# Prompt attention in a hybrid decoder layer: mask added inside VectorE's maximum, exponentials taken in place, copies and exponentials in turn on ScalarE

## The reference, cut to what matters

```python
s_own = jnp.einsum('tcgd,scd->tcgs', qg, k_own) * scale      # scale = 64 ** -0.5
s_own = jnp.where(causal[:, None, None, :], s_own, NEG_INF)
p = jax.nn.softmax(jnp.concatenate([s_sel, s_own], axis=-1), axis=-1)
o = einsum(p_sel, v_sel) + einsum(p_own, v_own)
```

## Time and profile before

| | |
|---|---|
| time, median of three runs | 3346.05 us |
| time of the profiled execution | 3341.74 us |
| its span | 3340.1 us, 51638 instructions |
| busy in the span | PE 3169.9 (95%), DVE 1574.2 (47%), ACT 548.8 (16%), POOL 249.3 (7%) |
| chain that ended last | PE 87%, DVE 5%, issue 3%, ACT 2% |
| attention of the prompt | from 959.5 to 1120.9 us |

### The profile page before, as it was taken

How to read it: one execution, slowest core, us unless ns; L and a number is a source line. 1 busy time by engine, 2 the same in 40 slices (tenths; PEclk the granted TensorE clock), 3 DMA queues, 4 the chain that set the end, 5 groups by cost and what they waited for, 6 DMA issues and landing times.

```text
span 3340.1 us, 51638 instructions
## 1 busy us (share of the span) xinstructions
PE 3169.9 (95%) x21384; PEld 2546.7 (76%) x21384; DVE 1574.2 (47%) x2674; ACT 548.8 (16%) x1222; POOL 249.3 (7%) x493
## 2 busy tenths in 40 slices
PE   8999899999978899897999999999999999999997
PEld 6888677887844566675888888888888877888886
DVE  4344466648976422226433443344334443443457
ACT  1000244422223433302000000000000001000012
POOL 0000011100000444400000000000000000000000
PEclk9999899999979999998999999999999999999998
DMA  5323000013210577821232233223323322222232
GB/s 166 82 77 88 18 11 10 10 49 79 63 33 7 175 236 250 252 90 44 83 86 78 80 85 88 77 81 83 88 76 83 82 83 81 75 84 82 81 92 78
DMA packets 445213, 289.32 MB, mean 87 GB/s; under 512 B 22809, under 2 KB 433926, under 8 KB 443576
## 3 DMA queue, kind: packets, MB, share of 16 engines
q1 hardware_dynamic: 430164, 244.44, 25.9%
q0 software_dynamic: 14816, 41.57, 3.9%
HBM read 275.46 MB, written 10.49 MB: 86 GB/s over the span
## 4 chain that ended last, share of the span: by engine, by line
PE 87%; DVE 5%; issue 3%; ACT 2%; DMA 1%; SPq 1%; POOLq 1%; POOL 0%; DVEq 0%; ACTq 0%
PE ps L1102 49%; PE ps L600 10%; PE ps L695 7%; PE ps L590 5%; PE ps L942 4%; PE ps L1081 3%; PE ps L930 1%; PE ps L905 1%; SPq L459 1%; POOLq L389 1%; PE ps L1038 1%; PE ps L908 1%; PE ps L999 1%; DVE BIG L1695 0%; ACT BIG L1337 0%
## 5 line engine op out<-in xcount | busy, mean ns | idle before, releaser
L1102 PE MATMUL ps<-XT,W 128*128 128x272 f32 x1408 | 339.5, 394 | 20.3 <-ACT XT L1425 19.7
L1102 PE MATMUL ps<-XT,SUMS 128*128 128x272 f32 x1408 | 337.0, 392 | 0.0
L1102 PEld LDWEIGHTS ps<-XT,W 128*128 128x128 f32 x1408 | 268.9, 191 | 77.2 <-issue 21.4
L2056 DVE TENSOR_TENSOR U2B<-ps,S1B 128x272 f32<-128x272 f32 x76 | 33.5, 441 | 615.7 <-PE ps L1102 615.7
L1102 PEld LDWEIGHTS ps<-XT,SUMS 128*128 128x128 f32 x1408 | 267.5, 190 | 55.1
L590 PE MATMUL ps<-XT,W 128*128 128x272 f32 (+1 forms) x832 | 193.4, 393 | 1.7 <-ACT XT L1192 0.9
L590 PEld LDWEIGHTS ps<-XT,W 128*128 128x128 f32 (+1 forms) x832 | 153.3, 184 | 43.6 <-issue 5.9
L1102 PE MATMUL ps<-TD,W 128*128 128x272 f32 x704 | 174.4, 397 | 5.9 <-DVE TD L1959 4.3
L1102 PE MATMUL ps<-BIG,SUMD 128*128 128x272 f32 x704 | 172.0, 393 | 4.2 <-ACT S5B L1453 4.2
L1102 PE MATMUL ps<-BIG,W 128*128 128x272 f32 x704 | 172.1, 393 | 2.4 <-ACT CNB L1431 2.4
L1102 PE MATMUL ps<-T3U,W 128*128 128x272 f32 x704 | 168.5, 392 | 0.0
(11 more groups left out here) (389 smaller groups left out, 4883.9 us busy)
## 6 DMA issues: line engine op xcount, KB each, us to landing
W<-in_w_up_dram SPq DMA_DIRECT2D x176, 512.0 KB, 5.2
W<-in_w_in_dram SPq DMA_DIRECT2D x38, 1024.0 KB, 5.8
W<-in_w_down_dram SPq DMA_DIRECT2D x64, 384.0 KB, 4.3
W<-in_w_down_dram SPq DMA_DIRECT2D x64, 320.0 KB, 3.8
W<-in_cache_k_dram SPq DMA_DIRECT2D x128, 128.0 KB, 3.5
W<-in_cache_k_dram POOLq DMA_DIRECT2D x128, 128.0 KB, 3.8
W<-in_cache_v_dram SPq DMA_DIRECT2D x128, 128.0 KB, 3.5
W<-in_cache_v_dram POOLq DMA_DIRECT2D x128, 128.0 KB, 3.6
```

Source lines behind the costliest of these rows:

```text
L1102: last = nc.tensor.matmul(ps[:, bank, 0:HALF], weights[:, k * P:(k + 1) * P], x[:, k], start=start and k == 0, stop=k == kc - 1, skip_grou ...
L2056: nc.vector.tensor_tensor(U2B, E, S1B, ALU.add).then_inc(S["u2_ev"], 1)
```

## The change

On TensorE the mask products are gone, the two loops are one loop over 16 heads (the scores of the next head are always issued ahead), and a bank is free when VectorE has read it. VectorE has a new constant `MASK` of 512 columns, 384 zeros and then the causal block. For a block it issues one `tensor_tensor_reduce`: it adds mask and scores, multiplies by -SCALE, writes that into `PR`, and the minimum of the row goes out as the bias of the exponential. It does so for head n + 1 behind the normalising of head n. ScalarE takes the exponentials in place in `PR`, and in the order exponential of block a of head n + 1, copy of group a of head n.

```diff
+        MASK = at("MASK", [P, 512], 19464)[:, :]
...
# TensorE
-                    for k, i in enumerate(BLOCKS):
-                        pe.wait_ge(S["pexp_ev"], 4 * n + k + 1)
-                        nc.tensor.matmul(ps[:, i, 0:(i + 1) * P], Q2[j][rows, f, i * P:(i + 1) * P], KC[j][rows, 0:(i + 1) * P],
-                                         start=True, stop=False, skip_group_check=True)
-
-                        nc.tensor.matmul(ps[:, i, i * P:(i + 1) * P], ident, const("causal"),
-                                         start=False, stop=True, skip_group_check=True).then_inc(S["sc_mm"], 1)
...
+                for k, i in enumerate(BLOCKS):
+                    if n:
+                        pe.wait_ge(S["max_ev"], 4 * n + k - 3)
+                    nc.tensor.matmul(ps[:, i, 0:(i + 1) * P], Q2[j][rows, f, i * P:(i + 1) * P], KC[j][rows, 0:(i + 1) * P],
+                                     start=True, stop=True).then_inc(S["sc_mm"], 1)
+            head_scores(0)
+            for n in range(16):
+                if n < 15:
+                    head_scores(n + 1)
+                pe.wait_ge(S["pnorm_ev"], n + 1)
...
# ScalarE
-                        nc.scalar.activation(PR[hd % 2][:, off:off + (i + 1) * P], ps[:, i, 0:(i + 1) * P], ACT.Exp,
-                                             bias=STAT[:, 4 + hd % 2, i:i + 1], scale=SCALE, accum_out=STAT[:, 6 + hd % 2, i:i + 1]).then_inc(S["pexp_ev"], 1)
...
+                x = PR[n % 2][:, off:off + (i + 1) * P]
+                nc.scalar.activation(x, x, ACT.Exp, bias=STAT[:, 4 + n % 2, i:i + 1], scale=-1.0,
+                                     accum_out=STAT[:, 6 + n % 2, i:i + 1]).then_inc(S["pexp_ev"], 1)
+            for k in range(4):
+                block_exps(0, k)
+            for n in range(16):
+                for a in range(4):
+                    if n < 15:
+                        block_exps(n + 1, a)
+                    act.wait_ge(S["pt_mm"], 4 * n + a + 1)
+                    toff = sum(4 - x for x in range(a)) * P
+                    nc.scalar.activation(PT[n % 2][:, toff:toff + (4 - a) * P], ps[:, 4 + a % 3, 0:(4 - a) * P], ACT.Copy).then_inc(S["pt_ev"], 1)
...
# VectorE
-                        nc.vector.tensor_reduce(STAT[:, 2 + b, i:i + 1], ps[:, i, 0:(i + 1) * P], AX, ALU.max).then_inc(S["att_chain"], 1)
-                        dve.wait_ge(S["att_chain"], 5 * n + k + 1)
-                        nc.vector.tensor_scalar(STAT[:, 4 + b, i:i + 1], STAT[:, 2 + b, i:i + 1], -SCALE, None, ALU.mult).then_inc(S["max_ev"], 1)
...
+            nc.vector.memset(MASK[:, 0:3 * P], 0.0).then_inc(S["att_chain"], 1)
+            nc.vector.tensor_copy(MASK[:, 3 * P:4 * P], const("causal")).then_inc(S["att_chain"], 1)
...
+            def masked_max(n):
+
+                if n >= 2:
+                    dve.wait_ge(S["pt_mm"], 4 * n - 4)
+                for k, i in enumerate(BLOCKS):
+                    dve.wait_ge(S["sc_mm"], 4 * n + k + 1)
+                    off = i * (i + 1) // 2 * P
+                    nc.vector.tensor_tensor_reduce(out=PR[n % 2][:, off:off + (i + 1) * P], in0=ps[:, i, 0:(i + 1) * P],
+                                                   in1=MASK[:, (3 - i) * P:4 * P], scale=-SCALE, scalar=3e38, op0=ALU.add, op1=ALU.min,
+                                                   accum_out=STAT[:, 4 + n % 2, i:i + 1]).then_inc(S["max_ev"], 1)
...
+            masked_max(0)
+            for n in range(16):
+                dve.wait_ge(S["pexp_ev"], 4 * n + 4)
+                nc.vector.reciprocal(STAT[:, 8 + b], STAT[:, 6 + b]).then_inc(S["att_chain"], 1)
...
+                l.then_inc(S["pnorm_ev"], 1)
+                if n < 15:
+                    masked_max(n + 1)
+                if n and b == 0:
+                    output(n // 2 - 1)
+                recur(1)
```

More of the change, by code:

```diff
@@ new lines, in head_scores @@
+            def head_scores(n):
+                f, e = divmod(n % 4, 2)
+                j = n // 4 % 2
+                rows = slice(e * 64, e * 64 + 64)
+                if n % 4 == 0:
+                    pe.wait_ge(S["stat_copy"], n // 4 + 1)
+                for k, i in enumerate(BLOCKS):
[3 more added lines that the diff above has]
+                                     start=True, stop=True).then_inc(S["sc_mm"], 1)
@@ new lines, in _ @@
+            head_scores(0)
+            for n in range(16):
+                e, j, b = n % 2, n // 4 % 2, n % 2
+                rows = slice(e * 64, e * 64 + 64)
+                if n < 15:
+                    head_scores(n + 1)
+                pe.wait_ge(S["pnorm_ev"], n + 1)
+                for a in range(4):
+                    pe.wait_ge(S["pt_ev"], 4 * n + a + 2)
+                    for i in range(a, 4):
+                        off = i * (i + 1) // 2 * P
+                        last = nc.tensor.transpose(ps[:, 4 + a % 3, (i - a) * P:(i - a + 1) * P], PR[b][:, off + a * P:off + (a + 1) * P], ident)
+                    last.then_inc(S["pt_mm"], 1)
+                if e == 0:
+                    pe.wait_ge(S["ao_ev"], n // 2 + 1)
+                for a in range(4):
+                    pe.wait_ge(S["pt_ev"], 4 * n + a + 4)
+                    toff = sum(4 - x for x in range(a)) * P
+                    last = nc.tensor.matmul(ps[rows, 7, a * P:512], VS[j][:, a], PT[b][:, toff:toff + (4 - a) * P],
+                                            start=a == 0, stop=a == 3, skip_group_check=True)
+                last.then_inc(S["ao_mm"], 1)
@@ L1327, in _, with block_exps @@
             nc.scalar.activation(QSW.rearrange("p f n -> p (f n)"), ps[:, 7, 0:256], ACT.Copy).then_inc(S["qsw_ev"], 1)
-            act.sem_inc(S["pexp_ev"], 4)
             act.sem_inc(S["pt_ev"], 3)
[L1331 to L1336, removed]
-                        nc.scalar.activation(PR[hd % 2][:, off:off + (i + 1) * P], ps[:, i, 0:(i + 1) * P], ACT.Exp,
-                                             bias=STAT[:, 4 + hd % 2, i:i + 1], scale=SCALE, accum_out=STAT[:, 6 + hd % 2, i:i + 1]).then_inc(S["pexp_ev"], 1)
[L1339 to L1347, removed]
+            def block_exps(n, k):
+                i = BLOCKS[k]
+                act.wait_ge(S["max_ev"], 4 * n + k + 1)
+                off = i * (i + 1) // 2 * P
+                x = PR[n % 2][:, off:off + (i + 1) * P]
[4 more added lines that the diff above has]
+            for n in range(16):
+                for a in range(4):
+                    if n < 15:
+                        block_exps(n + 1, a)
+                    act.wait_ge(S["pt_mm"], 4 * n + a + 1)
+                    toff = sum(4 - x for x in range(a)) * P
+                    nc.scalar.activation(PT[n % 2][:, toff:toff + (4 - a) * P], ps[:, 4 + a % 3, 0:(4 - a) * P], ACT.Copy).then_inc(S["pt_ev"], 1)
             act.sem_inc(S["sc_ev"], 4)
@@ L1794, in _ @@
             l.then_inc(S["qk_laid"], 1)
+            nc.vector.memset(MASK[:, 0:3 * P], 0.0).then_inc(S["att_chain"], 1)
+            nc.vector.tensor_copy(MASK[:, 3 * P:4 * P], const("causal")).then_inc(S["att_chain"], 1)
+            dve.wait_ge(S["att_chain"], 2)
             dve.sem_inc(S["ao_ev"], 1)
[L1797 to L1807, removed]
-                        nc.vector.tensor_reduce(STAT[:, 2 + b, i:i + 1], ps[:, i, 0:(i + 1) * P], AX, ALU.max).then_inc(S["att_chain"], 1)
-                        dve.wait_ge(S["att_chain"], 5 * n + k + 1)
-                        nc.vector.tensor_scalar(STAT[:, 4 + b, i:i + 1], STAT[:, 2 + b, i:i + 1], -SCALE, None, ALU.mult).then_inc(S["max_ev"], 1)
[L1811 to L1825, removed]
@@ new lines, in output @@
+            def output(q):
+                dve.wait_ge(S["ao_mm"], 2 * q + 2)
+                nc.vector.tensor_copy(ZT[:, q, 0:SEQ], ps[:, 7, :]).then_inc(S["ao_ev"], 1)
+            masked_max(0)
+            for n in range(16):
+                b = n % 2
+                dve.wait_ge(S["pexp_ev"], 4 * n + 4)
+                nc.vector.reciprocal(STAT[:, 8 + b], STAT[:, 6 + b]).then_inc(S["att_chain"], 1)
+                dve.wait_ge(S["att_chain"], n + 3)
+                for i in range(4):
+                    off = i * (i + 1) // 2 * P
+                    x = PR[b][:, off:off + (i + 1) * P]
+                    l = nc.vector.tensor_scalar(x, x, STAT[:, 8 + b, i:i + 1], None, ALU.mult)
+                l.then_inc(S["pnorm_ev"], 1)
[4 more added lines that the diff above has]
+                recur(1)
+                if n == 11:
+                    for j in (6, 7):
+                        dve.sem_inc(page_free[j], 1)
@@ L1827, in _ @@
+            output(7)
             dve.sem_inc(S["dec_ev"], 1)
```

## The result

The changed kernel takes 3307.16 us, the median of four runs (3301.69 to 3307.45); the kernel before takes 3346.38 in as many beside it. Ratio 0.988, 95% interval 0.9863 to 0.9898: faster by 39 us.

A forecast was written before the change was run, and what follows sets the result against it. TensorE, 87% of the last-ending chain, was taken to bound the kernel. Attention savings of 5.1, 1.4 and 24.8 us, together 31.3, gave 3310.4 from 3341.74, 3314.8 as median, written 3316; range 3309 to 3329.

The forecast's parts named there:

- Masks, four at 0.42 us: TensorE's scores in each attention head: dropping four mask products saves 1.68 us, leaving 2.73 of 4.41 us, taken as 2.8.
- Copies and exponentials in turn, 2.55 us: ScalarE's new order in each head: transposes to values take 1.99 + 0.56 = 2.55 us, against 2.45 before.
- That half of the change is worth nothing: ScalarE's alternation of copies and exponentials was claimed to gain nothing, minus 0.1 us a head.
- VectorE hidden, with 0.7 us at the tightest place: VectorE's load in an attention head, 6.4 of 7.65 us, stays hidden behind TensorE with some 0.7 us to spare.
- The alternating heads and the break: Late VectorE in every second recurrence head, the break between loops and one low-clock head: 5.2 us, gone with the single loop.
- Transfers: Key cache pages behind the attention stage still arrive in time; GpSimd's idle time falls from 13 to about 5 us, cost 0.
- The clock: TensorE's clock in the attention stage: up behind the first values, which come 5 us earlier, and then stays up.
- both rivals: Clock up one to three heads later, 3319 to 3328 us, chance 0.18; clock low for most of the stage, 3378, 0.04.
- The masked maximum at half rate: Rival: VectorE's masked maxima take 3.7 us a head and bind, giving back 4 to 10 us, 3319 to 3325; chance 0.13.
- From the profiled execution to the median: Whole kernel: the run median is 4.3 us above the profiled execution, so 3310.4 becomes 3314.8; written as 3316 for the clock.

## Why the prediction was off, step by step

- **Masks, four at 0.42 us: this step failed.** I read the price from the mask's own issue to the next, 1098.49 to 1098.91, and took only that out of the 4.41 us. The row itself shows more: "[0.76 <-issue]" in front of the mask is time in which its weights could not be loaded, because the rows change from 64 to 128, and that lengthens the score product ahead of it. The four masks of a head bring six changes of row count: 4 x 0.22 + 6 x 0.195 = 2.06 us a head, 0.515 us a piece, for 1.68. The 0.42 us held the bare product and the change behind it, and not the change ahead of it. I had even rounded the rest up to 2.8 us. From values 1 to values 14 that is 13 x (7.65 - 7.22) = 5.6 us; up to the first values, at the low clock, the stage fell from 19.24 to 11.98 us, 7.3 instead of 5.1, for the same reason (0.96 us a mask, not 0.72). Both together are the missing 7.8 us (39.1 against 31.3).
- **Copies and exponentials in turn, 2.55 us: right, 2.57.** "That half of the change is worth nothing" was right against the cycle of before (2.45) and wrong as a statement of what the edit does: with short scores the old order costs 19.4 us, 10.5 of them through the clock. The term in the sum was right, since it was built for the new cycle.
- **VectorE hidden, with 0.7 us at the tightest place: right, with more room.** 0.69 + 0.08 us a masked maximum of 512 columns against 0.79 taken, but the four overlap at their ends and fill 1.65 us a head for 2.35 taken; VectorE waits 1.15 us for the next scores, and its normalising ends 2.2 us before it is needed.
- **The alternating heads and the break: right in kind.** They are gone. Yet with the masks back in the new orders the whole kernel is no faster than before, and its stage only 2.3 us shorter. The parts don't add: masks alone 6.3 us (some 9 more went into the clock), orders and single loop alone 2.3, all together 39.1.
- **Transfers: right.** 4.11 us idle for the forecast 5, and nothing given back that the medians show; their interval, 34 to 46 us of gain, would hide 2 or 3 us.
- **The clock: right; both rivals fell.** It rose behind the first values, as before, and stayed up. With one wait less it rose with the first values themselves (first values 2.56 us, not 4.00), so its place is not fixed to a step of the program. In the experiments it fell where TensorE had idled for 1.4 us and more, but not each time. What decides it stays open.
- **The masked maximum at half rate** fell: 0.69 us for 512 columns. The sources, one in PSUM, don't show a halving. The Trainium skill ("Vector Engine (DVE) Microarchitecture Reference", "Points that are easy to get wrong") has it for two sources in SBUF; no run here has such a pair with an accumulator. Without one, `scalar_tensor_tensor` over two sources in SBUF took 0.785 us for 128x544 in the kernel before (L1515), which is not half the rate either.
- **From the profiled execution to the median.** I added 4.3 us and then 1.2 of caution toward a later clock. Against the medians the gain is 39.2, as in the stage.

## What to carry to other kernels

Price an instruction that you take out of TensorE's queue by the cycle with and without it, not by the time from its own start to the next one's: a short product whose row count differs from its neighbours' keeps their weight loads uncovered too (here 0.22 us of work, 0.515 us of time). Before crediting an edit with its price, look at what is late next in the old order; a saving on one engine and a better order on two others were worth 6 and 2 us apart and 39 together, partly because waits in the old orders let the clock fall. And check which copy each wait truly needs: a wait one too strict cost 13.6 us in a single line.

## What was unexpected of the hardware

- A change of row count between neighbouring products, 64 to 128 or back, costs TensorE 0.195 us at the full clock, in the same bank or another; two experiments that differ in the number of products give the same value. Either direction costs: from a mask's load to the next score's 0.42 us pass (1030.00 to 1030.42), 0.22 of work and the change behind it; the rest of a mask's price lengthens the score product ahead of it.
- An idle stretch of TensorE's matmuls of 1.4 us and more can be followed by values at the lower clock level (3.5 to 4.5 us for 2.37). Its length alone doesn't decide: 2.78 us before head 8 of the kernel before with one wait less left the clock up, while with ScalarE's old order 1.49 us in every head (1.73 by the rows of the loads) were followed by a fall in every second head. Up to 0.78 us between loads, as in the changed kernel, never was.
- `tensor_tensor_reduce` with one source in PSUM runs at the rate of a plain maximum, 0.69 us for 128x512, and its separate read of the minimum (0.08 us) costs nothing in a sequence.
